# Two expert layers on one core: row DMAs, clears, logits and choice in another order

## The chip, the core and the metric

The kernel runs on one core of a Trainium2 chip. The metric is the device time of one execution in microseconds, from the first to the last instruction with what lies around them. The core has a matrix engine (TensorE, PE in the profile), a vector engine (VectorE, DVE), a scalar engine (ScalarE, ACT), a general one (GpSimd, POOL) and one that only issues transfers (SyncE, SP). They run programs of their own and wait for each other by semaphores. POOL, ScalarE and SyncE each have a DMA queue; all queues are served by the same 16 DMA engines.

## What is computed

One step of a two-layer network on 384 tokens (128 of context, 256 latent), 1024 wide, in float32. Each layer is a mixer (layer 0: gated linear attention beside a spatial gate; layer 1: grouped-query attention), and behind it 32 gated experts, of which each token uses two. The change is in the experts:

```python
def hier_moe(h, w_rg, b_rg, w_re, b_re, w_g, w_u, w_d):
    ...
    g_prob = jax.nn.softmax((x @ w_rg + b_rg).astype(F32), axis=-1)
    g_p, g_i = lax.top_k(g_prob, 1)
    e_logits = (x @ w_re + b_re).astype(F32).reshape(-1, MOE_GROUPS, MOE_PER_GROUP)
    e_sel = jnp.take_along_axis(e_logits, g_i[:, :, None], axis=1)[:, 0]
    e_v, e_i = lax.top_k(e_sel, MOE_TOPK)
    gate = jax.nn.softmax(e_v, axis=-1) * g_p
    expert = g_i * MOE_PER_GROUP + e_i
    combine = jnp.sum(jax.nn.one_hot(expert, N_EXPERTS, dtype=F32) * gate[..., None], axis=1)
    hid = jax.nn.silu(jnp.einsum('nd,edf->nef', x, w_g)) * jnp.einsum('nd,edf->nef', x, w_u)
    hid = hid * combine[:, :, None].astype(hid.dtype)
    ...
```

Every sub-layer is also modulated: x + m[5] * y with h = norm(x) * (1 + m[4]) + m[3], where the rows m come from a product of the conditioning vectors with a 1024 x 6144 matrix (w_mod) a layer. Those products are made in chunks along the way, one chunk a modulation row.

## The kernel before

The 384 tokens are three blocks of 128. All weights come through a ring of six slots of 2 MB that SyncE fills in a fixed order, each slot as soon as its last user is done: first the chunks of w_mod and of the mixer's matrices, then the experts, two at a time (a pair): gate, up and down weights of pair 0 in slots 0 to 2, of pair 1 in 3 to 5, and so on. In layer 0 the last modulation chunks of the ring, called "router" and "places" after the stage in which they are made, hold slots 2, 3 and 4, 5 until they have been multiplied, summed, copied to rows (`rest_row_ready`) and stored to DRAM (`rest_stored`) by POOL's `store_rest`. `load_rows` then broadcasts stored rows to all 128 partitions: gate rows (1 MB, GT) and shift and scale rows (2 MB, GS).

An expert layer goes like this. TensorE transposes the normalised rows H and multiplies them with the router weights: 36 logits by 384 tokens, expert in the partitions. ScalarE adds the bias (L1202), TensorE transposes the logits back to one token a partition (L862), VectorE copies them (L1529) and chooses: group by maximum, the two best experts (L1546, L1549), the gates by exponentials of ScalarE (L1204, L1205), one-hot rows of the choice (L1565, L1566). TensorE counts with triangular and full matrices of ones how many tokens of an expert come before each (L869 to L873, in two accumulations), VectorE makes each token's place out of it (L1572 to L1584) and two comparison matrices (`in_slot`, `in_pair`, L1592 to L1595), whose product (L878) is a table: for every pair and slot the token and its gate. VectorE also clears the accumulator ACC, which lies in the buffer of the transposed rows (L1568). POOL reads the table's columns (L580) and fetches a pair's rows with an indirect DMA (L583, into XS), from a copy of H that ScalarE stored in DRAM (L1199). Rows with no token are not fetched, so XS is cleared first (L594).

Then the pairs run in a loop: rows transposed (L889), gate and up products (L915), SiLU, hidden transposed (L923), down product (L936), the result scaled and scattered back to tokens by a one-hot product (`to_token`, L903, L904), added to ACC (L1618). POOL fetches the rows two pairs ahead, SyncE refills the slots.

All orders are written out by hand, an engine at a time. POOL's queue is one: what it issues later stands behind what it issued earlier, and its program stops at each wait.

## Time and profile before

| what | value |
|---|---|
| median of three timed runs | 1107.22 us (1103.3 to 1109.07) |
| the profiled execution: time / span | 1106.28 / 1104.5 us |
| TensorE busy | 951.4 us, 86% of the span |
| VectorE / ScalarE / POOL busy | 465.3 / 222.7 / 93.4 us |
| moved by DMA | 303.86 MB, mean 275 GB/s |
| mean granted TensorE clock | 0.93 of 2.4 GHz |
| weights of a pair of experts, each of gate, up, down | 2048 KB |
| chain of waits: TensorE / VectorE / DMA / POOL | 75% / 12% / 3% / 1% |

Times of the trace are counted from the span's start. The expert layers begin at about 290 and 789 us, their loops run from about 378 to 590 and from 859 to 1071 us. The chain of waits is followed back from the last instruction, at each step to what released it; its rows give start, length and what it was. In timelines a row is start, length, engine, line, operation, tile written and read, shapes and count, and in brackets how long the engine had idled before and what ended that. The granted clock is a share of 2.4 GHz, so 0.50 is the 1.2 GHz level.

### The profile page before, as it was taken

Reading aid. Unit: us, or ns where it says so; the run is one execution under the profiler, and the core shown is the slowest. Engines: PE = TensorE matmul, PEld = TensorE weight load, DVE = VectorE, ACT = ScalarE, POOL = GpSimd, SP = SyncE. Lnnn points to the kernel's source line nnn. Section 1 sums busy time; section 2 is a strip of 40 time slices with the busy share of each in tenths; the row PEclk is TensorE's granted clock in tenths of the full one; section 3 lists DMA queues with packets and bytes.
Section 4 is the critical chain, followed back from the end, with each engine's and each line's share of the span. In section 5 each row is a group of like instructions: output and inputs, shape, how many; then the busy total and the mean of one; then the engine's idle time right before and its main releaser. Section 6 shows DMA issues by size and latency. Waiting matters only on the chain.

```text
span 1104.5 us, 11649 instructions
## 1 busy us (share of the span) xinstructions
PE 951.4 (86%) x4106; PEld 468.0 (42%) x4106; DVE 465.3 (42%) x926; ACT 222.7 (20%) x394; POOL 93.4 (8%) x155
## 2 busy tenths in 40 slices
PE   2899999889844999999998999889739999999980
PEld 0254455644432444444443456544434444444440
DVE  0133265642540345444446255632452444444454
ACT  0312221410301212212113213410302212212111
POOL 4010000110011000000000200010011000000000
PEclk9799999989966999999999899899858999999995
DMA  9992622272765999999999933020496999999931
GB/s 294 390 343 76 227 79 77 86 272 76 283 239 212 413 419 420 421 421 420 420 405 364 345 134 131 23 81 1 190 374 241 420 419 421 420 420 421 420 131 57
DMA packets 76006, 303.86 MB, mean 275 GB/s; under 512 B 9600, under 2 KB 9664, under 8 KB 50504
## 3 DMA queue, kind: packets, MB, share of 16 engines
q1 hardware_dynamic: 66296, 278.58, 64.0%
q0 software_dynamic: 8880, 21.74, 5.6%
q10 hardware_dynamic: 800, 3.15, 0.8%
q8 instruction: 19, 0.31, 0.1%
q14 instruction: 11, 0.09, 0.0%
HBM read 310.69 MB, written 5.32 MB: 286 GB/s over the span
## 4 chain that ended last, share of the span: by engine, by line
PE 75%; DVE 12%; ACT 4%; issue 3%; DMA 3%; SPq 2%; POOL 1%; DVEq 0%; ACTq 0%; POOLq 0%
PE psum L915 20%; PE psum L657 20%; PE psum L936 11%; PE psum L889 4%; DVE ht L1618 3%; PE psum L903 2%; PE psum L904 2%; PE psum L745 2%; PE psum L779 2%; PE psum L687 1%; PE psum L646 1%; DMA arena<-h_rows,arena 1%; PE psum L1007 1%; PE psum L856 1%; PE psum L923 1%
## 5 line engine op out<-in xcount | busy, mean ns | idle before, releaser
L657 PE MATMUL psum<-ring,ht 128*128 128x512 f32 (+1 forms) x576 | 232.0, 561 | 0.7 <-ACT ht L1053 0.7
L915 PE MATMUL psum<-ring,arena 128*64 128x512 f32 x1024 | 230.3, 603 | 1.5 <-ACT arena L1215 1.5
L657 PEld LDWEIGHTS psum<-ring,ht 128*128 128x128 f32 x576 | 108.6, 191 | 115.6 <-issue 110.9
L915 PEld LDWEIGHTS psum<-ring,arena 128*64 128x64 f32 x1024 | 76.1, 139 | 149.6 <-issue 149.6
L936 PE MATMUL psum<-ring,arena 128*64 128x512 f32 x512 | 116.9, 598 | 9.0 <-DVE ht L1618 8.0
L1618 DVE TENSOR_TENSOR ht<-ht,psum 128x512 f32<-128x512 f32 x192 | 117.7, 683 | 4.1 <-PE psum L904 2.0
L1656 DVE TENSOR_TENSOR arena<-arena,psum 128x256 f32<-128x256 f32 x32 | 13.5, 421 | 202.6 <-ACT arena L1221 202.6
L1643 DVE SCALAR_TENSOR_TENSOR y_low<-psum,arena,y_top 128x512 fp32r<-128x512 f32 x64 | 48.1, 751 | 83.6 <-ACT y_top L1228 83.6
L903 PE MATMUL psum<-y_top,to_token 128*128 128x512 f32 x192 | 78.6, 409 | 3.5 <-DVE y_low L1643 3.5
L1228 ACT ACTIVATE y_top<-psum,arena 128x512 fp32r<-128x512 f32 x64 | 44.1, 689 | 181.9 <-PE psum L936 181.9
L904 PE MATMUL psum<-y_low,to_token 128*128 128x512 f32 x192 | 75.2, 392 | 0.0
L687 PE MATMUL psum<-ring,cond_silu 128*32 128x512 f32 x384 | 51.1, 672 | 23.6 <-DMA ring<-in_w_mod 23.6
L936 PEld LDWEIGHTS psum<-ring,arena 128*64 128x64 f32 x512 | 34.3, 136 | 76.9 <-issue 56.0
L889 PE MATMUL psum<-ident,arena 128*128 128x128 f32 x272 | 41.1, 296 | 28.4 <-DMA arena<-h_rows,arena 28.4
L889 PEld LDWEIGHTS psum<-ident,arena 128*128 128x128 f32 x272 | 34.2, 196 | 55.2 <-DMA arena<-h_rows,arena 29.2
L1221 ACT ACTIVATE arena<-psum 128x256 f32<-128x256 f32 x32 | 12.3, 385 | 203.3 <-PE psum L915 203.3
L1215 ACT COPY arena<-psum 128x512 f32<-128x512 f32 x68 | 36.8, 591 | 53.2 <-PE psum L889 53.2
L903 PEld LDWEIGHTS psum<-y_top,to_token 128*128 128x128 f32 x192 | 36.2, 189 | 12.5 <-issue 5.3
L580 POOL CAST arena<-arena 128x1 uint32 (+1 forms) x36 | 6.7, 185 | 391.6 <-PE psum L889 391.5
L583 POOL DMA_INDIRECT arena<-h_rows,arena x36 | 36.5, 1015 | 31.4 <-POOL arena L580 29.0
L904 PEld LDWEIGHTS psum<-y_low,to_token 128*128 128x128 f32 x192 | 36.0, 188 | 6.7
L687 PEld LDWEIGHTS psum<-ring,cond_silu 128*32 128x32 f32 x384 | 11.8, 119 | 58.7 <-issue 45.3
(275 smaller groups left out, 839.7 us busy)
## 6 DMA issues: line engine op xcount, KB each, us to landing
ring<-in_w_exp_gate SPq DMA_DIRECT2D x32, 2048.0 KB, 14.0
ring<-in_w_exp_up SPq DMA_DIRECT2D x32, 2048.0 KB, 18.5
ring<-in_w_exp_down SPq DMA_DIRECT2D x32, 2048.0 KB, 16.5
ring<-in_w_mod SPq DMA_DIRECT2D x24, 2048.0 KB, 16.5
ring<-in_w_in_even SPq DMA_DIRECT2D x5, 2048.0 KB, 21.0
shift_scale<-mod_rows POOLq DMA_DIRECT2D x3, 2048.0 KB, 10.9
ring<-in_w_in_odd SPq DMA_DIRECT2D x3, 2048.0 KB, 21.4
ring<-in_w_out_even SPq DMA_DIRECT2D x2, 2048.0 KB, 9.0
```

The costliest lines, as they stand in the source:

```text
L583: pool.indirect_dma_start(XS[v], None, h_rows[l], bass.IndirectOffsetOnAxis(ap=from_row[v][:, 0:1].bitcast(U32), axis=0), bounds_check=T - ...
L657: mm = pe.matmul(psum[:, to, 0:cols], HT[:, k, b * P:(b + 1) * P], w[:, k, :], start=(k == 0), stop=(k == KC - 1))
L687: mm = pe.matmul(psum[32 * j:32 * j + 32, to, :], cond_silu[:, k, 2 - 2 * half:34 - 2 * half], w[:, k, :], start=(half == 0 and r == 0), s ...
L889: t = pe.transpose(psum[:, half, kk * P:(kk + 1) * P], XS[v][:, 4 * half + kk:D:KC], ident[:, :])
L903: pe.matmul(to, to_token[v][:, b * P:(b + 1) * P], Y_HI[:, cols], start=True, stop=False)
L904: pe.matmul(to, to_token[v][:, b * P:(b + 1) * P], Y_LO[:, cols], start=False, stop=True).then_inc(M("back_ps"), 1)
L915: mm = pe.matmul(psum[64 * e:64 * e + 64, 2, :], XT[:, k, 64 * e:64 * e + 64], RG[:, 3 * v:3 * v + 2, e, k, :], start=(k == 0), stop=(k == ...
L936: mm = pe.matmul(psum[64 * e:64 * e + 64, 4 + n, :], HTS[v][:, k, 64 * e:64 * e + 64], RD[:, 3 * v + 2, e, k, n * 512:(n + 1) * 512], star ...
L1215: act.copy(XT[:, 4 * half:4 * half + 4, :], bank(half).rearrange("p (k s) -> p k s", k=4)).then_inc(M("x_sb"), 1)
L1228: act.activation(Y_HI[:, n * 512:(n + 1) * 512], bank(4 + n), ACT.Copy, scale=token[v][:, 1:2]).then_inc(M("y_top"), 1)
L1618: dve.tensor_tensor(acc, acc, bank((6, 7, 4, 5, 6, 7)[c]), ALU.add).then_inc(M("added"), 1)
L1643: dve.scalar_tensor_tensor(Y_LO[:, cols], bank(4 + n), token[v][:, 1:2], Y_HI[:, cols], ALU.mult, ALU.subtract).then_inc(M("y_low"), 1)
```

## The change

- POOL: the clears of XS move ahead of the stores of the modulation rows; the first two row DMAs move ahead of the store of "places" and of the broadcasts; POOL no longer waits for `x_updated` and `h_ready` at the broadcasts, since the rows' store implies both.
- Logits: the transposed rows become the loaded operand and the router weights the streamed one, so that the logits come out by token; the bias is one more product (a row of ones with the bias row). ScalarE's copy and the transposes go.
- VectorE: the one-hot rows are made right behind the choice and sent to the counts; the gates come after the places. The counts are read from PSUM without a copy. The clear of ACC goes; the first pair's result is copied to it, not added.
- Counts: one accumulation of four products over 128, 96, 64 and 32 columns, with a fourth block of zeros for the total, in place of nine of 32 columns.
- TensorE in layer 0: "router" is multiplied before the counts as before, but summed after them; "places" is multiplied before the table product, and summed after it. The table goes to bank 7.

```diff
-        BR = vx(8)[0:36, 0:1]
+        BR = vx(40)[0:1, 0:36]
+        oh_sum = vx(4 * 32, "p (b n) -> p b n", b=4)
...
             def experts(l):
                 u = 2 * l + 1
...
+                if l == 0:
+                    pool.wait_ge(S("cat_ready"), 1)
+                    pool.wait_ge(S("stored"), 16 * 4)
+                for v in range(2):
+                    pool.memset(XS[v], 0.0).then_inc(M("rows_cleared"), 1)
+                pool.memset(oh_sum[:, NB, :], 0.0).then_inc(M("rows_cleared"), 1)
                 store_rest(f"norm_{u}")
                 if l == 0:
                     store_rest("router")
-                    store_rest("places")
-                pool.wait_ge(S("x_updated"), NB * u)
-                load_rows(u, (2, 3), gt_t[:, :], "gate_in")
-                if l == 0:
-                    pool.wait_ge(S("h_ready"), NB * (u + 1))
-                    load_rows(2, (0, 2), gs_t[:, :], "rows_in")
...
+                pool.wait_ge(M("rows_cleared"), 3)
+                pool.wait_ge(S("h_stored"), 16 * (l + 1))
                 pool.wait_ge(S("table_ready"), l + 1)
-                pool.wait_ge(S("h_stored"), 16 * (l + 1))
-                for v in range(2):
-                    pool.memset(XS[v], 0.0).then_inc(M("rows_cleared"), 1)
-                pool.wait_ge(M("rows_cleared"), 2)
-                for v in range(2):
-                    gather(v, v, static=True)
+                for q in range(2):
+                    gather(q, q, static=True)
+                if l == 0:
+                    store_rest("places")
+                load_rows(u, (2, 3), gt_t[:, :], "gate_in")
+                if l == 0:
+                    load_rows(2, (0, 2), gs_t[:, :], "rows_in")
...
                     transposed(u, b)
+                    to = psum[:, 7, b * 36:(b + 1) * 36]
                     for k in range(KC):
-                        mm = pe.matmul(psum[0:36, 6, b * P:(b + 1) * P], WR[:, k, :], HT[:, k, b * P:(b + 1) * P], start=(k == 0), stop=(k == KC - 1))
+                        pe.matmul(to, HT[:, k, b * P:(b + 1) * P], WR[:, k, :], start=(k == 0), stop=False)
+                    mm = pe.matmul(to, ones[0:1, :], BR, start=False, stop=True)
...
                 if l == 0:
-                    mod_group("router")
+                    mod_products(mods("router")[0])
+                pe.wait_ge(M("rows_cleared"), 3)
                 pe.wait_ge(S("chosen"), l + 1)
...
+                pe.matmul(psum[:, 6, 0:4 * 32], before[:, :], oh_sum, start=True, stop=False)
+                for a in range(NB):
+                    mm = pe.matmul(psum[:, 6, (a + 1) * 32:4 * 32], ones[:, :], oh_sum[:, a:a + 1, :].broadcast_to([P, NB - a, 32]),
+                                   start=False, stop=(a == NB - 1))
                 mm.then_inc(S("counts_ps"), 1)
...
+                if l == 0:
+                    mod_sum(mods("router")[0])
+                    mod_products(mods("places")[0])
...
                 if l == 0:
-                    mod_products(mods("places")[0])
                     mod_sum(mods("places")[0])
...
-                link(dve.memset(ht_t[:, :], 0.0))
...
+                        if first:
+                            dve.tensor_copy(acc, found).then_inc(M("added"), 1)
+                        else:
+                            dve.tensor_tensor(acc, acc, found, ALU.add).then_inc(M("added"), 1)
```

POOL's program where layer 0's experts begin, before: the product and store of "places", the two broadcasts (gate rows, shift and scale rows), the two clears of XS, and two times a table column read and a row DMA.

```order
L540 ISA
L540 TENSOR_TENSOR ring<-ring 4x512 [waits rest_row_ready,rest_stored]
L512 DMA mod_rows<-ring 2x512 [waits pool_steps]
L512 DMA mod_rows<-ring 2x512
L491 DMA gate_rows<-mod_rows 128x2048 [waits x_updated,rest_stored]
L491 DMA shift_scale<-mod_rows 128x4096 [waits h_ready]
L594 MEMSET arena 128x1024 [waits h_stored,table_ready]
L594 MEMSET arena 128x1024
L580 CAST arena<-arena 128x1 [waits moe0_rows_cleared]
L583 DMA arena<-h_rows,arena 128x1024 [waits moe0_row_looked_up]
L580 CAST arena<-arena 128x1
L583 DMA arena<-h_rows,arena 128x1024 [waits moe0_row_looked_up]
```

The same place now, from the store of "router" on:

```order
L511 DMA mod_rows<-ring 2x512 [waits rest_row_ready,rest_stored]
L511 DMA mod_rows<-ring 2x512
L580 CAST arena<-arena 128x1 [waits h_stored,table_ready,moe0_rows_cleared,rest_stored]
L583 DMA arena<-h_rows,arena 128x1024 [waits moe0_row_looked_up]
L580 CAST arena<-arena 128x1
L583 DMA arena<-h_rows,arena 128x1024 [waits moe0_row_looked_up]
L539 ISA
L539 TENSOR_TENSOR ring<-ring 4x512 [waits rest_row_ready]
L511 DMA mod_rows<-ring 2x512 [waits pool_steps]
L511 DMA mod_rows<-ring 2x512
L490 DMA gate_rows<-mod_rows 128x2048 [waits rest_stored]
L490 DMA shift_scale<-mod_rows 128x4096
```

The row DMAs moved ahead of the product, the store and the broadcasts of "places"; the clears stand earlier in the program, ahead of this piece.

VectorE's program in layer 0, before, from the difference of the two best logits over the gates to the one-hot rows and the clear of ACC (ht is its buffer):

```order
L1551 TENSOR_TENSOR arena<-arena 128x3 [waits dve_links]
L1554 TENSOR_REDUCE arena<-arena 128x3 [waits router_exp]
L1555 RECIPROCAL arena<-arena 128x3 [waits dve_links]
L1557 TENSOR_SCALAR arena<-arena 128x3 [waits dve_links]
L1558 RECIPROCAL arena<-arena 128x3 [waits dve_links]
L1559 TENSOR_TENSOR arena<-arena 128x3 [waits dve_links]
L1560 TENSOR_TENSOR arena<-arena 128x3 [waits dve_links]
L1561 CAST arena<-arena 128x6 [waits dve_links]
L1562 TENSOR_SCALAR arena<-arena 128x24 [waits dve_links]
L1565 TENSOR_TENSOR arena<-iota,arena 128x96 [waits dve_links] x2
L1566 TENSOR_TENSOR arena<-arena 128x96 [waits dve_links]
L1568 MEMSET ht 128x3072
```

The same place now, from the choice's index to the first readers of the counts in PSUM:

```order
L1549 CAST arena<-arena 128x6 [waits dve_links]
L1552 TENSOR_TENSOR arena<-iota,arena 128x96 [waits dve_links]
L1552 TENSOR_TENSOR arena<-iota,arena 128x96
L1554 TENSOR_TENSOR arena<-arena 128x96 [waits dve_links]
L1555 TENSOR_TENSOR arena<-arena 128x3
L1556 TENSOR_SCALAR arena<-arena 128x24
L1557 CAST arena<-arena 128x3x2 [waits dve_links]
L1558 SCALAR_TENSOR_TENSOR arena<-arena 128x3x2 [waits dve_links]
L1563 TENSOR_TENSOR arena<-arena,psum 128x96 [waits counts_ps,dve_links]
L1563 TENSOR_TENSOR arena<-arena,psum 128x96
```

The one-hot rows come right after the index; the gates' seven steps, which wait for ScalarE, are behind the places now, and the clear is gone.

TensorE's program in layer 0, before, from the sum of "router" over the nine count products to the table and the products of "places" (ring<-cond_silu):

```order
L705 MATMUL psum<-ring,pick 4x512 [waits rest_row_ready,mod_part_sb]
L706 MATMUL psum<-mod_bias,pick_bias 4x512
L870 MATMUL psum<-arena,before 128x32 [waits chosen,rest_row_ready]
L869 MATMUL psum<-arena,ones 128x32
L870 MATMUL psum<-arena,before 128x32
L869 MATMUL psum<-arena,ones 128x32 x2
L870 MATMUL psum<-arena,before 128x32
L873 MATMUL psum<-arena,ones 128x32 x3
L878 MATMUL psum<-arena 128x200 [waits entries_ready]
L878 MATMUL psum<-arena 128x200 x5
L687 MATMUL psum<-ring,cond_silu 32x512 [waits chunk_in_4,mod_part_sb]
L687 MATMUL psum<-ring,cond_silu 32x512 x7
```

The same place now:

```order
L869 MATMUL psum<-arena,before 128x128 [waits chosen,moe0_rows_cleared]
L871 MATMUL psum<-arena,ones 128x96
L871 MATMUL psum<-arena,ones 128x64
L871 MATMUL psum<-arena,ones 128x32
L708 MATMUL psum<-ring,pick 4x512 [waits rest_row_ready,mod_part_sb]
L709 MATMUL psum<-mod_bias,pick_bias 4x512
L690 MATMUL psum<-ring,cond_silu 32x512 [waits chunk_in_4,mod_part_sb]
L690 MATMUL psum<-ring,cond_silu 32x512 x7
L690 MATMUL psum<-ring,cond_silu 32x512 [waits chunk_in_5]
L690 MATMUL psum<-ring,cond_silu 32x512 x7
L880 MATMUL psum<-arena 128x200 [waits entries_ready]
L880 MATMUL psum<-arena 128x200 x5
```

The sum of "router" moved behind the counts, and the products of "places" from behind the table to ahead of it.

## Rows read from the trace of the kernel before

**Rows 1.** The chain of waits, 286 to 350 us (layer 0): start, length, what.
```profile
293.28 3.63 PE psum L856 x32
...
296.93 0.59 ACT arena L1202
...
297.97 0.28 DVE arena L1529
...
301.36 0.18 DVE arena L1551
...
301.90 0.18 DVE arena L1554
...
304.97 2.63 DVE ht L1568
...
308.03 0.27 DVE arena L1572
...
313.74 4.37 PE psum L878 x12
318.11 3.93 PE psum L687 x32
...
325.61 1.26 POOL ring L540
...
329.55 0.44 POOL gate_rows L491
...
334.05 10.76 DMA arena<-h_rows,arena
```

**Rows 2.** The chain of waits, 786 to 832 us (layer 1).
```profile
814.32 4.38 PE psum L878 x12
...
820.07 1.99 POOL arena L594 x2
...
823.20 3.33 DMA arena<-h_rows,arena
```

**Rows 3.** The chain of waits inside layer 0's loop: two gate/up products, two pairs apart.
```profile
408.21 6.87 PE psum L915 x32
...
438.45 6.87 PE psum L915 x32
```

**Rows 4.** DMA issues by tile, 357 to 390 and 540 to 575 us: count, size, us to landing.
```profile
ring<-in_w_exp_up SPq DMA_DIRECT2D x3, 2048.0 KB, 16.6
...
ring<-in_w_exp_up SPq DMA_DIRECT2D x1, 2048.0 KB, 20.8
```

**Rows 5.** The timeline of TensorE at the counts of layer 0.
```profile
304.74 0.39 PE L869 MATMUL psum<-arena,ones 128*128 128x32 f32 x2
...
305.31 1.04 PE L869 MATMUL psum<-arena,ones 128*128 128x32 f32 x4
```

**Rows 6.** Stretches: engines' busy times, granted clock, DMA share, GB/s in the last columns.
```profile
312.00:316.00 4.00, 2.26 (x7) 2.26 (x8) 2.20 (x7) 0.00 (x0) 0.00 (x0) 0.50 1.01 420
...
822.00:824.00 2.00, 0.00 (x0) 0.00 (x0) 0.13 (x1) 0.00 (x0) 1.03 (x3) 0.50 0.97 406
```

**Rows 7.** DMA issues, 420 to 450 and 780 to 840 us, and the timeline at 793.9.
```profile
arena<-h_rows,arena POOLq DMA_INDIRECT x2, 8.1
...
h_rows<-h ACTq DMA_DIRECT2D x1, 1536.0 KB, 16.8
...
793.90 0.38 ACTq L1199 DMA_DIRECT2D h_rows<-h  x1
```

**Rows 8.** The timeline of SyncE: pair 1's down weights, and the loop's first load.
```profile
329.28 0.37 SPq L420 DMA_DIRECT2D ring<-in_w_exp_down  x1
357.59 0.39 SPq L420 DMA_DIRECT2D ring<-in_w_exp_gate  x1
```

**Rows 9.** The timeline of VectorE: the same three steps without and beside a POOL clear.
```profile
319.71 0.68 DVE L1636 TENSOR_SCALAR to_token<-iota,arena 128x128 fp32r<-128x128 f32 x3
...
820.29 1.84 DVE L1636 TENSOR_SCALAR to_token<-iota,arena 128x128 fp32r<-128x128 f32 x3
```

More of the change, by code:

```diff
@@ L1550, in experts @@
                 link(a)
-                dve.tensor_tensor(top_f[:, :, 1:2], top_v[:, :, 1:2], top_v[:, :, 0:1], ALU.subtract).then_inc(S("router_sub"), 1)
+                link(dve.tensor_copy(top_f, top_i[:, :, 0:2].bitcast(U32)))
+                all32 = iota32.rearrange("p (o n) -> p o n", o=1).broadcast_to([P, NB, 32])
+                for j in range(2):
+                    a = dve.tensor_tensor(oh[j], all32, top_f[:, :, j:j + 1].broadcast_to([P, NB, 32]), ALU.is_equal)
+                link(a)
@@ new lines, in experts @@
+                dve.wait_ge(S("counts_ps"), l + 1)
+                count = psum[:, 6, 0:NB * 32].rearrange("p (b n) -> p b n", b=NB)
+                for j in range(2):
+                    a = dve.tensor_tensor(oh[j], oh[j], count, ALU.mult)
+                link(a)
+                for j in range(2):
+                    a = dve.tensor_reduce(pos[:, j, :], oh[j], AX.X, ALU.add)
+                link(a)
+                p6 = pos.rearrange("p j b -> p (j b)")
+                shape = [P, 6, MAX_ROUNDS - 1]
@@ new lines, in experts @@
+                after_round = iota[:, 1:MAX_ROUNDS].rearrange("p (i k) -> p i k", i=1).broadcast_to(shape)
+                dve.scalar_tensor_tensor(slot_p, odd, float(HALF), p6, ALU.mult, ALU.add)
+                link(dve.scalar_tensor_tensor(passed, p6.rearrange("p (i k) -> p i k", k=1).broadcast_to(shape), 1.0 / HALF, after_round, ALU.mult, ALU.is_ge))
+                link(dve.tensor_reduce(i_a, passed, AX.X, ALU.add))
+                dve.scalar_tensor_tensor(slot_c, i_a, float(PAIRS), ef, ALU.mult, ALU.add)
@@ L1552, in experts, with along, across @@
+                link(dve.scalar_tensor_tensor(slot_p, i_a, float(-HALF), slot_p, ALU.mult, ALU.add))
+                def along(v, n):
+                    return v.rearrange("p (i n) -> p i n", n=1).broadcast_to([P, 6, n])
+                def across(n):
+                    return iota[:, 0:n].rearrange("p (i n) -> p i n", i=1).broadcast_to([P, 6, n])
                 dve.wait_ge(S("router_exp"), l + 1)
@@ L1555, in experts @@
                 link(dve.reciprocal(g_prob, g_sum))
-                e1 = top_f[:, :, 0]
+                e1 = rival[:, :, 0]
                 link(dve.tensor_scalar(g_sum, e1, 1.0, None, ALU.add))
```

75 lines of the change are left out of this document (19 added, 56 removed).

## Prediction

> **What bounds the kernel now.** I read the page first (TensorE is busy in nearly every slice but for the two stretches where the experts begin), then the chain of waits through those two stretches, then the chain inside the expert loop, then the DMA landing times. In the first layer the chain [rows 1] runs from the logits through VectorE's choice (297.97 on) and the table product (313.74) into the products of the next modulation chunk "places" (318.11). From there nothing on it serves the experts: POOL scales and stores that chunk (325.61), issues two broadcasts (329.55), clears the row buffers, and only at 334.05 issues the first row DMA, which lands 10.76 us later because 3 MB of broadcast stand ahead of it in POOL's queue. TensorE gets rows at 344.81, 26.7 us after the table product ended (318.11). In the second layer no modulation chunk and only one early broadcast are in the way: table product, 1.99 us of clears, a row DMA of 3.33 us [rows 2].
>
> Inside the loop TensorE sets the pace: two pairs of experts take 438.45 - 408.21 = 30.24 us, 6.87 of which is one gate/up product [rows 3]. A weight slot is refilled when its gate/up ends and needed two pairs later less one product, so 30.24 - 6.87 = 23.4 us later. The "up" weights land 16.6 us after issue at the loop's start and 20.8 at its end [rows 4]: DMA is a little slower than TensorE and loses 4.2 us over the loop, which the 23.4 just cover. 2.6 us are left, and that caps how much DMA may be put into the loop.
>
> **The change, first layer.** *Logits by token.* The same passes in another shape (128 columns loaded and 36 streamed, in place of 36 and 128), plus three bias products (six passes); ScalarE's biased copy and the three transposes go, 296.93 to 297.97 = 1.04 us [rows 1]. The old form takes 3.63 / 32 = 0.113 us a pass. The nearest rows to the new form are the counts, 128x32: two passes take 0.39 with their end, four take 1.04 (0.26 each) a moment later [rows 5]. I take 0.113: six passes 0.7, gain 0.3. Bounds: bias free, +1.0; 38 passes at 0.26, 9.9 for 3.63, a loss of 5.2.
>
> *VectorE, choice first.* From the copy of the logits to the table product are 313.74 - 297.97 = 15.8 us [rows 1]. Off it go: the wait for ScalarE's exponentials, 301.90 - 301.36 = 0.5 (they are asked for after the choice and are ready long before they are used; the gates' arithmetic moves behind the counts and costs there what it cost before); the clear of the accumulator, 2.63, which held the counts' reader until 308.03, 3.1 us after the clear began at 304.97; the copy of the counts, 0.3; the index shift and two links, some 0.5. In place of the clear VectorE waits for four count products (eight passes where there were eighteen), 0.9 at 0.113 to 2.1 at 0.26, of which its own small steps cover some: 0.9 net. Sum 3.5 (2.5 to 4.4). Table product ready to start at 313.74 - 0.3 - 3.5 = 309.9. The first add-back becomes a copy of the same tile and I cost that at nothing.
>
> *TensorE's order.* "router" is now summed after the counts and the products of "places" stand ahead of the table product, so they end at the earliest near 308.7 (3.93 at the speed of row 318.11) and at the latest near 312.5 (twice that, at the 1.2 GHz level). The table took 4.37 at a granted clock of 0.50, the 1.2 GHz level, right after TensorE had idled [rows 1, 6]; now it follows 16 matmuls. Best: 309.9 + 2.2 (2.4 GHz) = 312.1; worst: 312.5 + 4.4 = 316.9; I take 313.5, products half slow, table fast. The table's way through VectorE to POOL is 820.07 - 818.70 = 1.4 [rows 2]: POOL wakes at 314.9.
>
> *POOL.* The chunk's sum, store, both broadcasts and the clears no longer stand ahead. From the end of the clear to the issue are 823.20 - 822.06 = 1.1 [rows 2]: issue at 316.0. Landing: 3.33 with the weights drained [rows 2], 8.1 in the loop under weight traffic [rows 7], 10.76 behind the broadcasts [rows 1]. Two weight loads (4 MB, ten us at 420 GB/s, [rows 6]) will be in flight until about 322, so I take 7.0: rows at 323.0 in place of 344.81, **21.8 us** earlier (bounds 26.9 and 17.3; 14.6 with the landing of 10.76).
>
> The Trainium skill (DMA: Bandwidth & Descriptors, section Queues, rings and completion order) says that each DMA engine takes the queues in turn, packet by packet, so a short transfer in POOL's own queue need not wait for SyncE's. By that the rows would land almost as if alone. The 8.1 us of the loop speak against it, the 10.76 behind POOL's own broadcasts speak for the part that one queue is served in order.
>
> *What was hidden comes back as DMA.* The last weight load of the two first pairs waits for the store of "places" (329.28 before, [rows 8]), and the broadcasts follow that store. Now the store stands behind two row DMAs on POOL: 316.0, some 3 for the two issues (an estimate: the 1.1 twice and the issues themselves), 329.28 - 325.61 = 3.7 for the product and the store, 2.5 (a guess) for its place behind the rows: 325.2. Then 2 + 3 MB, 12.4 us at 420 GB/s, keep DMA busy until 338 (an estimate). The loop's first load comes 357.59 - 344.81 = 12.8 after the rows [rows 1, 8], at 336, and finds 2 us of old work; before it found none. Of the 2.6 us of slack this leaves little; with the rows of two more row DMAs I charge **1.5 us** (bounds: nothing; all 12.4 less 2.6 = 9.8).
>
> *Clears early.* POOL's two clears move to where POOL idles: in the first layer right behind the shift broadcast, beside VectorE's copies of the transposed mixer output; three VectorE steps beside such a clear took 1.84 in place of 0.68 [rows 9], so 0 to 1.2 us, under a whole block of products that TensorE still has to do: nothing. In the second layer they lie under the output projection: nothing.
>
> The Trainium skill (SBUF — State Buffer, section Who interferes with whom) has POOL and some VectorE instructions exclude each other at a shared port. [Rows 9] agree. It speaks against the change: the row DMA's descriptors would now be written beside just those three steps, up to 0.7 later a layer, and the sum would be 1.4 worse.
>
> **Second layer.** Logits 0.3, VectorE 2.9 (as above, counts at 0.26 a pass), clears 1.99: issue about 5 us earlier, at 818.2. The rows' store was issued at 793.90 and took 16.8, so 810.7, in time [rows 7]. But the weights of the first two pairs are still on their way: DMA is 0.97 busy at 822 to 824 [rows 6]. With the 1 MB broadcast now behind the rows they end some 2.5 earlier, near 821; landing 4.8 in place of 3.33. **3.5 us** gained (bounds 4.9 with 3.33; 0.1 with 8.1). The late broadcast ends before the loop's first load.
>
> Sum: 21.8 - 1.5 + 3.5 = 23.8. The profiled execution took 1106.28 us (span 1104.5), which gives 1082.5; the median of the three timed runs is 1107.22, 0.1% more, and gives 1083.4. I say **1083**.
>
> **Rivals.** *Rows land as if alone*: the weight loads in flight do not hold a short transfer of another queue; landing 3.33, so 3.7 more in the first layer, 1.4 in the second; DMA's slack takes 1 to 2 of it back. 1079. For: the second layer's 3.33. Against: 8.1 in the loop. (The rule of the Trainium skill named above would give this case.) *The loop becomes DMA's*: store and broadcasts slip by some 5 us more, most of the 5 MB falls into the loop, and from the middle of the first layer's loop TensorE waits for weights. Price 8 to 9.8 in place of 1.5: 1090. For: 20.8 of 23.4 at the loop's end. *The rows are not earlier*: POOL is held ahead of its first row DMA by something that was covered before, the landing of the "router" store or of the row store. Then only VectorE's part remains, 3.8 + 3.5: 1099. Against: the second layer's row store took 16.8 under fuller DMA [rows 7], so the first layer's, issued under the logits (293.28), is there by 310; and the "router" store, at 3.7 like that of "places", by 311. *Slower*: POOL's third row DMA stands behind the broadcasts as the first did before. TensorE asks for it at the end of the second gate/up product, some 25 us after the first rows, near 348, and 20 us after its issue; the worst landing shown is 10.76. From 348 on each us costs one, and to end 0.5% above before it would have to land near 377: 1112.
>
> **How the numbers follow.** Forecast 0.62, rows as if alone 0.14, DMA's loop 0.14, not earlier 0.06, slower 0.04. The range takes in the first three with their bounds: best 26.9 less 2 of slack, plus 4.9, is 1077; worst 14.6 - 1.5 + 0.1 is 1093. I give 1076 to 1093. About 0.5% (5.5 us) is what a measurement of this kernel can tell from no change. Not earlier at 1099 is half in, half outside of that: faster 0.93, same 0.03, slower 0.04.
>
> **What would show it.** In the chain of the first layer no broadcast, clear or "places" store between the table and the first row transposes; that transpose near 323 and the table's step to POOL near 315. The row DMA's landing between 3.3 and 8.1. "Up" landing near 23 us by the end of the first layer's loop, and at most short TensorE waits for weights there; in the second layer as before. The forecast is wrong if the first rows arrive after 330, if the table product starts after 313, or if waits for weights in the first loop sum to over 5 us.

## The result, and the profile after

The changed kernel takes 1088.59 us (median of four runs, 1087.42 to 1091.04) where the kernel before took 1106.73 on the same chip: a ratio of 0.9844 (95% interval 0.9816 to 0.9871), 18 us or 1.6% faster. That lies in the range of the prediction and on its side, but 5.6 us above the forecast of 1083, and two of the three signs that were to show the forecast wrong are there: the first rows reach TensorE after 330 (330.79), and the table product starts after 313 (318.58). The third is not: in the first layer's loop the trace has no wait of TensorE for weights. The profiled execution has a span of 1085.9 us beside 1104.5.

The chain of waits of the changed kernel, in order of time (start, duration, engine, tile, line, count). L860 is the logits' products, L861 their bias products, L690 the products of a modulation chunk (the first one is "router"), L869 the counts, L880 the table, L890 the transposes of the rows; from 771 on it is the second layer:

```profile
core 0 of [0], span 1085.9 us
...
291.07 3.26 PE psum L860 x16
294.33 0.57 PE psum L861 x2
...
304.76 6.45 PE psum L690 x32
311.21 0.42 PE psum L869 x2
...
318.58 2.31 PE psum L880 x12
...
323.51 7.24 DMA arena<-h_rows,arena
...
330.79 1.98 PE psum L890 x8
...
567.43 22.98 DMA ring<-in_w_mod
590.46 3.64 PE psum L690 x16
...
771.32 3.26 PE psum L860 x16
...
797.74 4.38 PE psum L880 x12
...
804.65 3.34 DMA arena<-h_rows,arena
...
808.04 1.99 PE psum L890 x8
```

Beside [rows 1] and [rows 2]: the store, the broadcasts and the clears are off the chain. From the table's end to the issue of the row DMA it now takes 323.51 - 320.89 = 2.6 us. The row DMA itself lands after 7.24 in the first layer and 3.34 in the second. New on the chain are "router", whose products take 6.45 us and hold the counts, and, behind the loop, the landing of a chunk of w_mod for the next stage. The logits have no wait among them; it is the products that are long.

The windows of the changed kernel over its logits (length, busy time of PE, PEld, DVE, ACT, POOL with counts, granted clock, DMA share, GB/s):

```profile
290.00:296.00 6.00, 6.00 (x30) 5.86 (x30) 1.86 (x2) 1.19 (x3) 0.00 (x0) 0.51 0.82 291
296.00:302.00 6.00, 6.00 (x29) 5.86 (x27) 0.00 (x0) 2.44 (x3) 0.00 (x0) 0.50 1.01 359
302.00:308.00 6.00, 6.00 (x29) 3.34 (x32) 2.83 (x19) 0.00 (x0) 0.00 (x0) 0.50 0.48 195
308.00:314.00 6.00, 6.00 (x39) 2.01 (x35) 3.01 (x18) 1.37 (x4) 0.00 (x0) 0.79 0.78 281
```

and the same of the kernel before:

```profile
290.00:296.00 6.00, 6.00 (x48) 5.48 (x47) 0.00 (x0) 1.08 (x2) 0.00 (x0) 0.88 0.58 229
296.00:302.00 6.00, 4.83 (x44) 1.82 (x41) 3.24 (x21) 2.30 (x5) 0.00 (x0) 1.00 1.01 363
```

In the first window TensorE is busy for 6.00 of 6.00 us in both kernels, but before, it was granted 0.88 and then 1.00 of its clock; now it stays at 0.50, the 1.2 GHz level, for some 18 us. That a product of this shape can go with a low clock was on view in the kernel before, at its counts (128 columns loaded, 32 streamed), whose rows gave the prediction its bound of 0.26 us a pass:

```profile
304.00:308.00 4.00, 3.48 (x18) 3.42 (x18) 3.30 (x5) 0.35 (x1) 1.00 (x2) 0.63 1.01 428
```

Two executions differ before and between the changed stages too, so spans alone mislead. The table counts each stage from the start of its own first logits product, by the starts of the instructions in each kernel's trace. "Logits" is VectorE's copy of them, "table" the first table product, "rows" the first transpose of rows; "next stage" is TensorE's first product after the first layer's experts and update. The kernels below the second are the experiments.

| kernel | layer 1: logits | table | rows | next stage | layer 2: logits | table | rows |
|---|---|---|---|---|---|---|---|
| before | 8.8 | 24.6 | 55.7 | 325.5 | 9.7 | 25.5 | 37.7 |
| changed | 13.9 | 27.7 | 39.9 | 310.0 | 13.9 | 26.6 | 36.9 |
| logits by token alone | 13.9 | 30.4 | 60.7 | 330.6 | 13.9 | 29.7 | 42.0 |
| row DMAs first alone | 8.8 | 24.5 | 39.6 | 309.5 | 9.4 | 25.2 | 35.4 |
| choice first alone | 8.8 | 20.7 | 49.2 | 322.3 | 9.7 | 22.4 | 37.2 |
| changed, old logits | 7.7 | 19.6 | 33.1 | 306.6 | 9.4 | 22.1 | 35.3 |
| changed, three copies streamed | 8.8 | 20.6 | 34.9 | 308.9 | 9.8 | 22.4 | 35.0 |
| old logits, rows ahead of weights | 7.7 | 19.6 | 29.0 | 306.6 | 8.7 | 21.4 | 31.7 |
| old logits, no broadcasts | 8.9 | 20.8 | 35.1 | 306.5 | 9.4 | 22.1 | 35.1 |
| changed, 3.15 MB more | 13.9 | 27.3 | 40.1 | 319.4 | 13.9 | 26.6 | 36.8 |
| old logits, early gate, one hold | 7.7 | 19.6 | 33.0 | 303.5 | 9.4 | 22.1 | 32.4 |
| old logits, early gate, two holds | 8.5 | 20.4 | 30.4 | 303.6 | 9.3 | 22.0 | 32.3 |

The changed kernel gains 325.5 - 310.0 = 15.5 us in the first layer and 37.7 - 36.9 = 0.8 in the second, 16.3. The profile's 18.6 is made of that, less 1.7 that it arrived late at the first logits product (taken for chance: ahead of it the diff touches only the router's small loads and POOL's clears, and the twelve profiles arrive there at 289.2 to 292.1), and plus 3.9 gained between the two layers, where nothing is changed: the attention ran at another clock. The windows over the same work, first before, then changed, show it (third figure from the end):

```profile
684.00:704.00 20.00, 15.24 (x68) 11.06 (x69) 8.23 (x20) 11.55 (x35) 1.10 (x2) 0.74 0.35 118
```

```profile
670.00:690.00 20.00, 14.41 (x82) 10.36 (x81) 11.35 (x24) 12.51 (x39) 1.10 (x2) 1.00 0.35 118
```

From the next stage's first product to the second layer's first logits product the twelve profiles took 168.8 us at a mean granted clock of 0.985 to 174.2 at 0.951. There is one profile of each kernel, so whether such a difference belongs to the kernel or to the execution is not shown by them; but ten executions of one kernel, choice first alone, took from 1096.08 us at a mean clock of 0.939 to 1104.83 at 0.925. Differences of 2 or 3 us between kernels are therefore read from the table, not from spans.

The table has chance in it too. The old logits are the same products in eight rows of it, and take 7.7 to 8.9 us in the first layer: where they take 7.7, TensorE was granted 1.00 from the first of them on; in the others its clock had fallen to 0.50 at their start and rose within the first block. About 1 us of a difference at the logits is of this kind.

### The profile page after: what moved, and what is told of

The parts are those of the page before. It is cut to its first block, busy times and chain, and to the rows that moved or that the text cites. A ratio compares the mean times of both kernels' runs of the same rounds, so it can differ in the third digit from the quotient of the medians.

```text
span 1085.9 us, 11617 instructions
## 1 busy us (share of the span) xinstructions
PE 956.7 (88%) x4092; PEld 473.2 (44%) x4092; DVE 456.8 (42%) x922; ACT 221.2 (20%) x392; POOL 92.2 (8%) x157
## 3 DMA queue, kind: packets, MB, share of 16 engines
q10 hardware_dynamic: 800, 3.15, 0.7%
## 4 chain that ended last, share of the span: by engine, by line
PE 74%; DVE 10%; DMA 5%; issue 4%; ACT 4%; SPq 1%; DVEq 0%; POOL 0%; ACTq 0%; POOLq 0%
PE psum L916 21%; PE psum L660 21%; PE psum L937 10%; DMA ring<-in_w_mod 4%; PE psum L890 3%; DVE ht L1621 3%; PE psum L690 3%; PE psum L748 2%; PE psum L860 2%; PE psum L782 2%; PE psum L649 2%; PE psum L924 1%; PE psum L1032 1%; DMA arena<-h_rows,arena 1%; PE psum L904 1%
## 5 line engine op out<-in xcount | busy, mean ns | idle before, releaser
L1621 DVE TENSOR_TENSOR ht<-ht,psum 128x512 f32<-128x512 f32 x180 | 110.2, 680 | 4.0 <-PE psum L905 2.0
L690 PE MATMUL psum<-ring,cond_silu 128*32 128x512 f32 x384 | 57.5, 745 | 26.3 <-DMA ring<-in_w_mod 26.3
L890 PE MATMUL psum<-ident,arena 128*128 128x128 f32 x272 | 41.0, 296 | 14.3 <-DMA arena<-h_rows,arena 14.3
L890 PEld LDWEIGHTS psum<-ident,arena 128*128 128x128 f32 x272 | 34.1, 195 | 41.1 <-issue 26.0
L1213 ACT COPY arena<-psum 128x512 f32<-128x512 f32 x68 | 36.7, 589 | 35.3 <-PE psum L890 35.3
L904 PEld LDWEIGHTS psum<-y_top,to_token 128*128 128x128 f32 x192 | 36.2, 188 | 12.5 <-issue 5.3
L690 PEld LDWEIGHTS psum<-ring,cond_silu 128*32 128x32 f32 x384 | 12.6, 128 | 64.8 <-issue 48.4
L905 PEld LDWEIGHTS psum<-y_low,to_token 128*128 128x128 f32 x192 | 36.2, 188 | 6.9
```

Of the source, the lines that this page charges most:

```text
L690: mm = pe.matmul(psum[32 * j:32 * j + 32, to, :], cond_silu[:, k, 2 - 2 * half:34 - 2 * half], w[:, k, :], start=(half == 0 and r == 0), s ...
L890: t = pe.transpose(psum[:, half, kk * P:(kk + 1) * P], XS[v][:, 4 * half + kk:D:KC], ident[:, :])
L904: pe.matmul(to, to_token[v][:, b * P:(b + 1) * P], Y_HI[:, cols], start=True, stop=False)
L905: pe.matmul(to, to_token[v][:, b * P:(b + 1) * P], Y_LO[:, cols], start=False, stop=True).then_inc(M("back_ps"), 1)
L1213: act.copy(XT[:, 4 * half:4 * half + 4, :], bank(half).rearrange("p (k s) -> p k s", k=4)).then_inc(M("x_sb"), 1)
L1621: dve.tensor_tensor(acc, acc, found, ALU.add).then_inc(M("added"), 1)
```

## The experiments

**The logits put back.** The forecast missed 6 us at the first rows (39.9 where 55.7 - 21.8 = 33.9 was forecast); the low clock in the windows was the first suspect, the DMA debt the second.

```
-  to = psum[:, 7, b * 36:(b + 1) * 36]
   for k in range(KC):
-      pe.matmul(to, HT[:, k, b * P:(b + 1) * P], WR[:, k, :], ...)
-  mm = pe.matmul(to, ones[0:1, :], BR, start=False, stop=True)
+      mm = pe.matmul(psum[0:36, 6, b * P:(b + 1) * P], WR[:, k, :], HT[:, k, b * P:(b + 1) * P], ...)
...
+  act.activation(LT, psum[0:36, 6, 0:T], ACT.Identity, bias=BR)...
```

> The changed kernel with the logits alone put back (experts in the partitions, 36 columns loaded and 128 streamed, ScalarE's biased copy, three transposes). Theory C (clock): in the changed kernel TensorE works through the token-wise logits without a pause, yet its granted clock stays at 0.50, the 1.2 GHz level, from 290 to 308, where the kernel before had it rise within the first block; the logits end 4.9 us later in the first layer and 4.1 in the second than they would have, and the products of the chunk router behind them run at half speed, which costs 2 more in the first layer. Then this kernel shows a granted clock near 1.0 by the second block, and takes 1088.6 - 11 = 1077.6 us (1076 to 1081). Rival D (debt): what is missing of the forecast lies in the DMA work moved into the first loop; then the logits' form is worth under 1 us and the time stays at 1088. Rival S (slack): the logits end earlier as C says, but the first loop, which now starts 7 us earlier, waits for weights and keeps only the second layer's 4: 1084.

1084.17 us, ratio 0.9807 (0.9763 to 0.9851). The logits are there 13.9 - 7.7 = 6.2 us earlier, the rows 6.8 earlier, 33.1. So theory C (the clock) holds for the rows; some 1.1 of the 6.2 (8.8 less 7.7) goes with the clock that this run had at its first product. The time is that of rival S (the loop gives it back), though not by its split, which kept nothing of the first layer and 4 of the second: of the 6.8 the first layer keeps 310.0 - 306.6 = 3.4; its loop, from the first gate/up product to the last, is 234.5 long in place of 233.3, and from the last gate/up product to the next stage are 36.2 in place of 34.1. In the second layer of 4.5 us gained at the logits 1.6 reach the rows. The chain of waits of this kernel at the two row DMAs shows why:

```profile
316.42 8.55 DMA arena<-h_rows,arena
...
325.02 1.98 PE psum L893 x8
...
798.01 6.22 DMA arena<-h_rows,arena
...
804.28 1.99 PE psum L893 x8
```

Counted from the layer's first logits product they are issued 8.1 and 4.5 us earlier than in the changed kernel, and take 1.3 and 2.9 us longer to land: they come out among the weights of the second pair. In the second layer the last of these weights lands at 804.08, and the row DMA at 804.23.

**The logits alone.** The same form of logits put into the kernel before, without the rest.

> The kernel before with the logits by token alone. Theory C: 4.9 us lost in the first layer and 4.1 in the second, 1106.7 + 9 = 1115.7, at a granted clock of 0.50 through both logits. The prediction's own term (0.113 us a pass): 0.3 gained in each layer, 1106. Its upper bound (38 passes at 0.26): 5.2 lost in each, 1117.

1114.26 us, ratio 1.0076 (1.0044 to 1.0107): 8 us slower. The table has 13.9 - 8.8 = 5.1 lost at the first layer's logits and 4.2 at the second's, and both arrive whole at the rows (5.0 and 4.3): the row DMAs take 10.82 and 3.34 us to land, as before (10.76 and 3.33). The part of the change that the prediction called a gain of 0.3 a layer costs some 9 in both.

**Is it the clock, or the size of a pass?** The changed kernel, with the 36 columns streamed three times over in each pass (the bias products too; the first copy alone is read).

```
-  to = psum[:, 7, b * 36:(b + 1) * 36]
+  to = psum[:, 7, b * 108:(b + 1) * 108]
-  pe.matmul(to, HT[:, k, b * P:(b + 1) * P], WR[:, k, :], ...)
+  pe.matmul(to, HT[:, k, b * P:(b + 1) * P], WR[:, k:k + 1, :].broadcast_to([P, 3, 36]), ...)
```

> The changed kernel with its logits by token as they are, but each pass streams the router's 36 columns three times over (108 in place of 36; only the first copy is read): three times the streaming for the same result. Theory C (clock): the passes took 0.204 to 0.22 us because TensorE stayed at a granted clock of 0.50, not because of their size; with 108 columns streamed the clock rises as it did with 128, the passes shrink toward 0.113, the logits end some 4 us earlier in each layer, and the products of the chunk router run at full speed: about 1084, the time of the kernel with the old logits (1084.2). Rival L (load): a pass is bound by the loading of its 128 columns whatever is streamed; then the clock stays at 0.50, nothing moves, and the time is 1088.6; if the streams add up at the low clock, 24 columns-thirds more, up to 1093.

1084.08 us, ratio 0.9779 (0.9733 to 0.9825). Three times the streaming takes the logits from 13.9 to 8.8 us. Its windows over the logits:

```profile
290.00:296.00 6.00, 6.00 (x43) 5.79 (x42) 1.28 (x2) 2.68 (x5) 0.00 (x0) 0.81 0.51 209
296.00:302.00 6.00, 6.00 (x54) 3.79 (x57) 2.21 (x12) 0.85 (x1) 0.00 (x0) 1.00 0.99 356
```

TensorE is as busy as in the changed kernel, with the same loads, and is granted 0.81 and 1.00 in place of 0.51 and 0.50. The instructions of the logits' line (minimum/median/maximum ns), in the changed kernel:

```profile
L860 PEld LDWEIGHTS psum<-arena,ht x96: 287/333/338, 290.7 to 784.0; 128*128 128x128 f32 x96
```

and with three copies:

```profile
L860 PEld LDWEIGHTS psum<-arena,ht x96: 186/192/337, 290.5 to 778.8; 128*128 128x128 f32 x96
```

The load of 128 columns falls from 333 ns to 192 as the clock rises. Rival L (a pass bound by its load, whatever is streamed) falls: at the higher clock the new form, at 8.8 us, is within the old form's 7.7 to 8.9. What was lost is the clock.

**The row DMAs first, alone**, in the kernel before: POOL clears early, issues the two row DMAs as soon as the table is there, then stores "places" and issues the broadcasts. The rest is as before.

> The kernel before with POOL's part alone: row buffers cleared early, the first two row DMAs issued ahead of the store of places and of the broadcasts. Table product ends at 318.1 as before, POOL wakes 1.4 later, issues 1.1 later, landing 7: first rows at 327.6 in place of 344.8, 17 us; second layer 2 for the clears. Theory C, with the prediction's 1.5 us of DMA debt: 1106.7 - 17.5 = 1089. If the debt takes 5 or more: 1093 or later, with waits for weights in the first loop.

1085.02 us, ratio 0.9806 (0.9788 to 0.9825): this part alone gains at least as much as the whole change. The first layer's rows come at 39.6 in place of 55.7 and all 16 us reach the next stage (309.5 beside 325.5): the 5 MB that now go into the loop cost nothing here. The second layer gains 2.3: the clears' 2.0, and 0.3 that stand already at the logits.

**The choice first, alone**: old logits, POOL's old order.

> The changed kernel with the old logits and with POOL's old order (store of places, broadcasts and clears of the row buffers ahead of the row DMAs): what remains is VectorE's choice sent first, the four count products, the cleared accumulator gone, and the products of places ahead of the table. First layer: VectorE 3.5, the table at the full clock 2, the products of places 3.9 out of the way of POOL's store: rows some 9 earlier. Second layer: 2.9 by the prediction; but the kernel with the old logits and the row DMAs first got its second-layer rows at 37.2 us after the first transposes of the logits, whether VectorE's choice was first (804.28 - 767.07) or not (805.42 - 768.10 = 37.3), so theory W (the rows cannot land before the weights of the first two pairs) says 0 to 2. W: 1106.7 - 10 = 1097. The prediction's terms: 1094.

1101.11 us, ratio 0.9941 (0.9918 to 0.9964). From logits to table it is 11.9 us in place of 15.8 in the first layer and 12.7 in place of 15.8 in the second: 3.9 and 3.1 earlier. The first layer's rows come 6.5 earlier, of which 3.2 reach the next stage. In the second layer 3.1 us at the table are 0.5 at the rows: the row DMA takes 6.09 us in place of 3.33. This is what theory W (the rows cannot land before the weights of the first two pairs) expects. Together with the row DMAs first the choice is worth 0.1 there: 35.4 without it, 35.3 with it.

**Rows ahead of the weights.** To see whether the weights in flight hold the rows, one weight load of the second pair waits in each layer for the first row DMA, in the kernel with the old logits.

```
   before_first(3 * u + a)
+  if 3 * u + a == (4, 5)[l]:
+      sp.wait_ge(S(f"moe{l}_gathered_0"), 16)
   load_experts(l, a, 2 * u, 3 * u + a)
```

> The kernel with the old logits and the rest of the change, in which SyncE holds one of the six first weight loads of each layer (the second pair's up in the first layer, its down in the second) until the first row DMA has landed. Theory W: the row DMA landed 8.55 us after its issue in the first layer and 6.22 in the second because 2 to 4 MB of weights were queued ahead of it; held back, it lands after 3.3 to 4: rows 4.5 earlier in the first layer, 2.5 in the second. Of that the first loop gives back 2 to 4, since its weights start later against the rows and it had little slack (its length was 234.5 us beside 233.3 before): 1084.2 - 4 = 1080. Rival: the landing is the row DMA's own time beside any traffic (it took 8.1 in the loop): rows no earlier, 1084 or later.

1081.64 us, ratio 0.9768 (0.9722 to 0.9815). The first layer's rows come at 29.0 in place of 33.1, the second's at 31.7 in place of 35.3 (0.7 of these 3.6 stand already at the logits). The row DMAs land in 4.47 and 3.31 us in place of 8.55 and 6.22. Theory W holds: held weights, early rows. In the first layer nothing is kept (306.6 both times), and the chain shows what is late next:

```profile
329.93 17.56 DMA arena<-h_rows,arena
...
347.53 1.16 PE psum L895 x8
...
795.01 3.31 DMA arena<-h_rows,arena
...
798.36 1.98 PE psum L895 x8
```

The third row DMA, issued behind POOL's two broadcasts, takes 17.56 us (12.5 in the changed kernel). TensorE's waits for rows behind the first ones, 325 to 570 us (total, times, longest):

```profile
PE psum L895 <- DMA arena<-h_rows,arena: 2.3, 1, 2.3
```

With that wait the pair takes 18.5 us in place of 15.1. That is the mechanism of the prediction's slower rival. The last seven pairs of the loop together take 0.9 more than with the old logits alone, with "up" weights landing 23.1 us after issue. Of the second layer's 3.6 the loop gives back 1.2.

**What the broadcasts cost in the loop.**

```
-  load_rows(u, (2, 3), gt_t[:, :], "gate_in")
+  load_rows(u, (2, 3), gt_t[:, :], "gate_in", 8)
-      load_rows(2, (0, 2), gs_t[:, :], "rows_in")
+      load_rows(2, (0, 2), gs_t[:, :], "rows_in", 8)
```

> The kernel with the old logits and the rest of the change, but the broadcasts of gate, shift and scale rows that were put behind the row DMAs load 8 columns in place of 1024 and 2048 (the rest of these rows is left out, so older values are used): 3 MB less in the first layer's loop, 1 MB in the second's. It measures the debt that moving them into the loop makes. The prediction's charge: 1.5 us, so 1082.7. If the debt is real and large (the broadcasts take 7 us of DMA time from a loop with 2.6 of slack): the first loop 4 us or more shorter and 1080 or less. If the loop hides it all: 1084, and the first loop's 234.5 us stay.

1081.59 us, ratio 0.9756 (0.9711 to 0.9801). The loop is 233.5 in place of 234.5. From the rows to the next stage it takes 306.5 - 35.1 = 271.4, beside 273.5 with the broadcasts: 2.1 us. The total hardly moves (306.5 and 306.6), since this run's rows came 2.0 later, 1.2 of it at its logits. The kernel with three copies has the broadcasts and its rows at 34.9, and ends at 308.9, 2.4 later. The part of it that the loop shows is clear. The last "up" loads of the loop, us to landing, in the kernel before, the changed one, with the old logits, without the broadcasts, and with the choice first alone:

```profile
ring<-in_w_exp_up SPq DMA_DIRECT2D x1, 2048.0 KB, 20.8
...
ring<-in_w_exp_up SPq DMA_DIRECT2D x1, 2048.0 KB, 22.1
...
ring<-in_w_exp_up SPq DMA_DIRECT2D x1, 2048.0 KB, 21.9
...
ring<-in_w_exp_up SPq DMA_DIRECT2D x1, 2048.0 KB, 20.9
...
ring<-in_w_exp_up SPq DMA_DIRECT2D x1, 2048.0 KB, 20.9
```

With the old logits they had reached 23.0 a little earlier, and three pairs there take 15.6, 15.4 and 15.8 us from one gate/up product to the next, where the kernel before and the one without broadcasts take 15.0 and 15.2 in turn. The last five steps are 77.2 us long with the old logits, 76.1 in the changed kernel, 75.7 before and without the broadcasts. So the broadcasts cost up to 1.5 us in the loop when the rows are early. What comes behind the loop is not shown to be theirs: there the trace has a wait for a chunk of w_mod in every kernel but one, and 1.6 over the 269.8 of before remain even without broadcasts.

**As much DMA again.** The changed kernel, with a copy of 3.15 MB issued by SyncE behind the last of the six first loads.

```
+  if l == 0:
+      w = d["w_exp_gate"][1][0:3].rearrange("e (p k) n -> e p (k n)", p=P)
+      sp.dma_start(spare, w).then_inc(S("again"), 16)
```

> The changed kernel with 3.15 MB more of DMA in the first layer: behind the last of the six first weight loads SyncE copies three matrices of the second layer's experts to an unused place in DRAM, as much again as the broadcasts that the change moved behind the row DMAs. Theory W: DMA could end the first layer's stage at 306.5 us after its first logits product, the changed kernel ends at 310.0, so 3.5 us are free, and 3.15 MB at 420 GB/s take 7.5: 4 lost, 1092.5, with waits of TensorE for weights or for the chunk of norm_2 at the loop's end. If the loop has room for the broadcasts twice over: 1088.6. If it had none for the first 3 MB: 7.5 lost, 1096.

1098.81 us, ratio 0.9926 (0.9902 to 0.995): 9.4 us lost in the first layer (319.4), more than theory W's 4 and than all of the 7.5 us of DMA time. The chain:

```profile
335.57 26.87 DMA arena<-h_rows,arena
...
501.58 22.94 DMA ring<-in_w_exp_up
```

and TensorE's waits from 300 to 610 us (total, times, longest):

```profile
PE psum L895 <- DMA arena<-h_rows,arena: 15.7, 2, 9.0
```

The third row DMA needed 26.87 us, and TensorE stood for 15.7 - 9.0 = 6.7 until it had landed. The pair that waits for it takes 24.1 us in place of 15.1, which is nearly all of the 9.4; later the chain goes through a weight load. So the estimate of 3.5 us of free DMA time was not tested cleanly: the extra megabytes came in ahead of the one small transfer on which the loop hangs.

**A version from this.** Old logits, the rest of the change, the first layer's gate broadcast back into DMA's idle stretch (behind the store of "norm_1"), and the hold in the second layer alone; and the same with the hold in the first layer too.

```
   store_rest(f"norm_{u}")
   if l == 0:
+      pool.wait_ge(S("x_updated"), NB * u)
+      load_rows(u, (2, 3), gt_t[:, :], "gate_in")
       store_rest("router")
...
+  if l == 1 and 3 * u + a == 5:
+      sp.wait_ge(S(f"moe{l}_gathered_0"), 16)
   load_experts(l, a, 2 * u, 3 * u + a)
```

> The kernel with the old logits and the rest of the change, with two moves: the gate rows' broadcast of the first layer goes back ahead of the row DMAs, right behind the store of norm_1, into a stretch where DMA has idle time before the table; and in the second layer SyncE holds the last of the six first weight loads until the first row DMA has landed. Theory W: from the first logits product to the next stage's first product the first layer took 306.6 us with its rows at 33.1 and 306.6 with its rows at 29.0, so DMA sets that end; 1 MB less in the loop takes 2.5 us at 420 GB/s off it: 304. The second layer's rows come 31.7 after its first logits product in place of 35.3, of which 2.4 were kept. 1084.2 - 2.5 - 2.4 = 1079. If DMA does not set the first layer's end, that move is worth nothing: 1082.

> The same, with the hold in the first layer too (the second pair's up waits for the first row DMA). Theory W: rows at 29 after the first logits product, but the end of the stage is DMA's and the hold adds idle DMA time: 304 again, time as with one hold, 1079 (1078 to 1081). If TensorE sets the end of the stage: 4 us better than with one hold, 1075.

One hold: 1076.93 us, ratio 0.9736 (0.9708 to 0.9763), below both kernels. Two holds: 1080.87, ratio 0.9772 (0.9746 to 0.9797). The first layer ends at 303.5 and 303.6 us, with its rows at 33.0 and at 30.4. Against the old logits with rows at 33.1, 1 MB less in the loop goes with 3.1 us, 1.0 in the loop and 2.0 behind it. Rows 2.6 earlier are worth nothing: the loop is 2.6 longer, its late pairs take 15.4 to 15.8 us, and "up" lands after 23.0. The 4 us between the two medians are not in the stages of the table (equal in the second layer to 0.1); the two profiles differ by 2.3 between the layers and 1.7 ahead of them. The chain of the kernel with one hold, second layer:

```profile
786.42 4.38 PE psum L888 x12
...
793.32 3.33 DMA arena<-h_rows,arena
...
796.70 1.99 PE psum L898 x8
```

The row DMA is issued as early as with the old logits alone, and lands in 3.33 where it took 6.22.

## Why the prediction came out as it did, by its own steps

- **Logits by token: the step that failed.** Said: 0.113 us a pass, 0.3 gained in each layer. Measured: 5.1 lost in the first, 4.2 in the second. The prediction had the bound (a loss of 5.2, from [rows 5]) and chose the other end, because the count of passes is the same. The 0.113 came from a stretch that ran at the full clock, and the new form never got that clock: its 16 passes of a block took 3.26, 0.204 each. The bias products, priced as passes, took 0.57 each. That the bound is so near is in part luck: its 38 passes leave out the first block (the 32 of [rows 1] are two blocks of three), and its 0.26 is more than a pass took. The copy and the transposes that went away had cost 1.04.
- **What followed from it, in no term.** The low clock lasts into the "router" products: 6.45 us, beside 3.64 for the same 32 passes in the kernel before, from 297.86 on. The choice was there before they ended, and the counts waited: 13.8 from logits to table in place of 11.9. Of VectorE's gain 1.9 was lost.
- **VectorE, choice first: right.** Said 3.5 and 2.9; 3.9 and 3.1 with the old logits. That it would reach the rows holds in the first layer only. In the second the weights set the rows: 0.1 to 0.5 us of 3.1.
- **TensorE's order: right.** The table took 2.31 in place of 4.37 behind the products of "places", as taken.
- **POOL: right.** Issue 2.6 us after the table (2.5 said), landing 7.24 (7.0 said). This is the bulk of the change, 16 of the 21.8. The issue was sized from the right rows; the landing is in part luck. It was taken for an issue at 316.0; the kernel with the old logits issued at 316.42 and landed in 8.55, and 7.24 belongs to an issue at 323.51. The 3.33 of [rows 2] was also not one "with the weights drained": the last weight load of the first two pairs was issued at 788.82 and landed at 826.24, 0.3 ahead of that row DMA. The 0.7 a layer that a shared port might have cost the issue did not come: from POOL's read of the table's column to the issue it takes 1.1 us, as before.
- **The DMA debt: charged 1.5, measured 0.3.** From rows to next stage 269.8 before and 310.0 - 39.9 = 270.1 after. The loop's last five steps are 0.4 longer than before. The forecast of 21.8 in the first layer put the rows at 34. With its rows at 33.1 the old-logits kernel gives 3.4 us back: 1.2 in the loop, of the size that was charged, and 2.1 behind it, which are not shown to be debt. The sign of "up" landing near 23 us came: 22.1 to 22.5 in the loop's last three pairs.
- **Clears early: nothing, as said, in the first layer.** There they run from 236.35 to 238.2, and the two VectorE copies beside them take 0.69 us each, as before.
- **Second layer: said 3.5, measured 0.8.** VectorE 3.1 and the clears 2.0 against 4.2 of logits. The landing of 4.8 was taken for an early issue; it was 3.34 because the slow logits made the issue late, and 6.22 when they were fast. With the old logits the layer's rows come 37.7 - 35.3 = 2.4 earlier; there the landing is the term that was too small, by 1.4.
- **The rivals.** "The loop becomes DMA's" gives 1090, nearest to the 1088.6, and is not what happened: the loop took 233.3 us, as before, and no wait for weights is in it. A number near the result is no proof of its mechanism. "As if alone" falls in the first layer (7.24). "Not earlier" falls: POOL issued 2.6 us after the table. The slower rival's transfer landed 12.5 us after its issue and cost nothing; two experiments brought it out.

In sum: 15.5 in the first layer and 0.8 in the second, 16.3, where 23.8 were forecast. That the time missed by 5.6 and not by 7.5 is luck: where nothing was changed the two profiles differ by another 3.9 - 1.7 = 2.2. At the first layer's rows 15.8 were gained where 21.8 were forecast: of the 6.0 missing the logits are 5.4, the held counts 1.9, issue and landing 0.3, less 0.4 that VectorE gained more and 1.3 for a table that had only its entries to wait for.

What stays open: the stretch from the last gate/up product to the next stage took 33.5 to 37.1 us in the twelve profiles. Part of it is a wait for the next stage's weight chunk, but 37.1 also occurred where the rows came late (choice first alone). There the second chunk of w_mod took 26.5 us to land, in the kernel before 24.0, though "up" landed in 20.9 and 20.8 at the end of both loops. So DMA's backlog is not all of it, and what else slows these chunks is not shown.

## What to carry to other kernels

Price a product at the clock it will get, not by its count of passes: when a change swaps the sides of a product, look for a row of the new shape, take its rate as the forecast when it is the only one, read the clock that was granted there, and let that clock last into the work behind. When a wait is removed ahead of a stage fed by DMA, follow the next transfers in each queue (here the rows among the weights, then the third row DMA behind the broadcasts) and count an earlier start only up to the point from which DMA sets the stage's end. Compare stages from their own first instruction.

## What the runs showed of the hardware

- A TensorE busy 6.00 of 6.00 us stayed at a granted clock of 0.50 for 18 us with 128 columns loaded and 36 streamed a pass, and was granted 1.00 with the same loads and 108 streamed. More work was faster: 8.8 in place of 13.9 us.
- The first row DMA took 3.3 to 3.4 us in the second layer where the weights had landed, were held, or landed within 3.1 us of its issue, and 5.6 to 9.4 in either layer beside longer loads on another queue. Where the last of these landed 5.4 to 7.9 us after its issue (seven cases, the changed kernel's first layer among them), it landed 0.16 to 0.19 us behind that load. Where the last one had 9.9 to 11.0 us to go (four cases), it landed ahead of it: with the old logits it was issued at 316.42 and landed at 324.97, while a weight load issued at 312.99 landed at 326.4. This agrees with the Trainium skill (DMA: Bandwidth & Descriptors, section Queues, rings and completion order), by which the DMA engines take the queues in turn; but taking turns is not landing as if alone. In POOL's own queue the third row DMA, behind 3 MB of broadcasts, took 12.5 us in the changed kernel and 26.9 with 3.15 MB more on SyncE's; without the broadcasts it took 6.8.
- The unchanged stretch between the two layers took 168.8 us at a mean granted clock of 0.985 and 174.2 at 0.951 in twelve profiles: 5.4 us, as much as the term that the forecast missed.
